# Last token tile of a decoder layer: the row store issued ahead of a ring load and of the h store

## What is computed

```
h  = x + concat(attn_o, conv_o) @ w_out
hn2 = rms_norm(h, ffn_norm_gain)
out = h + sum over a token's 2 experts e of  weight_e * ( (silu(hn2 @ w_gate[e]) * (hn2 @ w_up[e])) @ w_down[e] )
```

## Time and profile before

| what | value |
|---|---|
| median of 3 runs | 1155.69 us |
| the 3 runs | 1153.41 to 1156.58 us |
| the profiled execution, its time | 1153.28 us |
| the profiled execution, its span | 1151.4 us |
| TensorE busy | 1089.9 us (95%) |
| VectorE busy | 852.5 us (74%) |
| DMA, mean over the span | 220 GB/s |

### The profile page before, as it was taken

The page is one execution under the profiler, slowest core; times in us unless marked ns, Lnnn a source line. Parts: engine busy times, 40 slices in busy tenths (PEclk is TensorE's granted clock), DMA queues, the critical chain, the costliest instruction groups (busy, mean ns, idle before and its releaser), DMA issues.

```text
span 1151.4 us, 15392 instructions
## 1 busy us (share of the span) xinstructions
PE 1089.9 (95%) x5617; PEld 856.9 (74%) x5617; DVE 852.5 (74%) x1208; ACT 679.4 (59%) x1003; POOL 357.1 (31%) x433
## 2 busy tenths in 40 slices
PE   5999999999879998989799999999999999999996
PEld 4999999889758877767567777777777777766664
DVE  6645354454677776767788998988988989888894
ACT  7424232231465655543477787787877877777773
POOL 2323333233421111121214424434344344222221
PEclk9999999999999999999699999999999999999998
DMA  8021030302311222324899999999999999999972
GB/s 246 2 61 50 19 93 1 92 19 92 123 12 37 75 92 92 129 92 154 308 356 367 372 375 374 371 376 376 368 377 378 369 368 363 367 358 366 374 314 56
DMA packets 77403, 253.64 MB, mean 220 GB/s; under 512 B 18832, under 2 KB 43408, under 8 KB 52752
## 3 DMA queue, kind: packets, MB, share of 16 engines
q1 hardware_dynamic: 70160, 235.85, 55.1%
q0 software_dynamic: 7168, 16.79, 6.2%
HBM read 240.03 MB, written 20.97 MB: 227 GB/s over the span
## 4 chain that ended last, share of the span: by engine, by line
PE 46%; DMA 8%; DVE 4%; ACT 2%; issue 1%; POOL 1%; POOLq 0%; SPq 0%; ACTq 0%; DVEq 0%
PE banks L2123 9%; PE banks L2125 9%; PE banks L2124 9%; DMA raw<-in_w_gate 6%; PE banks L2142 4%; PE banks L2146 4%; PE banks L2144 4%; PE banks L2099 2%; PE banks L1659 1%; PE banks L1661 1%; PE banks L1660 1%; PE banks L2108 1%; DMA xn_rows<-hn 1%; DVE wlo L2043 1%; PE banks L1689 1%
## 5 line engine op out<-in xcount | busy, mean ns | idle before, releaser
L2043 DVE TENSOR_TENSOR wlo<-raw,whi 128x2048 fp32r<-128x2048 f32 x190 | 428.1, 2288 | 47.6 <-ACT whi L1992 47.4
L1992 ACT CAST whi<-raw 128x2048 fp32r<-128x2048 f32 x188 | 354.0, 1910 | 33.6 <-DMA raw<-in_w_gate 19.9
L1974 POOL DMA_INDIRECT out<-y_sb,table_i x32 | 152.7, 4772 | 195.4 <-ACT y_sb L2010 190.8
L2123 PE MATMUL banks<-whi,rT_hi 128*96 128x512 f32 x512 | 206.7, 404 | 3.2 <-DVE wlo L2043 2.5
L2125 PE MATMUL banks<-whi,rT_lo 128*96 128x512 f32 x512 | 203.0, 396 | 0.0
L2124 PE MATMUL banks<-wlo,rT_hi 128*96 128x512 f32 x512 | 201.8, 394 | 0.0
L2123 PEld LDWEIGHTS banks<-whi,rT_hi 128*96 128x96 f32 x512 | 83.0, 162 | 38.0 <-issue 3.3
L2125 PEld LDWEIGHTS banks<-whi,rT_lo 128*96 128x96 f32 x512 | 82.9, 162 | 36.4
L2124 PEld LDWEIGHTS banks<-wlo,rT_hi 128*96 128x96 f32 x512 | 83.4, 163 | 31.5
L1965 POOL DMA_INDIRECT rows<-xn_rows,table_i x30 | 48.9, 1630 | 180.8 <-PE banks L2099 173.2
L874 ACT ACTIVATE qk_sq<-banks 128x256 f32<-128x256 f32 x32 | 12.3, 385 | 128.9 <-PE banks L1517 128.9
(11 more groups left out here) (250 smaller groups left out, 2064.6 us busy)
## 6 DMA issues: line engine op xcount, KB each, us to landing
raw<-in_w_gate SPq DMA_DIRECT2D x64, 1024.0 KB, 22.9
raw<-in_w_up SPq DMA_DIRECT2D x64, 1024.0 KB, 23.2
raw<-in_w_down SPq DMA_DIRECT2D x64, 1024.0 KB, 24.4
c_raw<-in_w_in SPq DMA_DIRECT2D x12, 512.0 KB, 3.8
q_raw<-in_w_in SPq DMA_DIRECT2D x12, 512.0 KB, 6.1
x_stage<-in_x SPq DMA_DIRECT2D x8, 512.0 KB, 6.4
wo_raw<-in_w_out SPq DMA_DIRECT2D x2, 2048.0 KB, 7.7
h_sb<-in_x SPq DMA_DIRECT2D x8, 512.0 KB, 4.9
```

The costliest lines, as they stand in the source:

```text
L1974: pool.indirect_dma_start(out=s.out_rows, out_offset=bass.IndirectOffsetOnAxis(ap=s.table_i[:, e:e + 1], axis=0), in_=s.y_sb[e % 2][:], in ...
L1992: act.copy(s.w_hi[i % HI][:], s.raw[i % RING][:]).then_inc(s.hi_ready, 1)
L2043: dve.tensor_tensor(s.w_lo[i % RING][:], s.raw[i % RING][:], s.w_hi[i % HI][:].bitcast(F32), ALU.subtract).then_inc(s.lo_ready, 1)
L2123: pe.matmul(o, s.rT_hi[e % 2][:, c, :], hi[:, c4, :], start=(c == 0), stop=False)
```

## The change

In the last position (i = 7) SP's queue waits for `hn_ready` and stores `hn` first, then waits for the last part of the output projection and loads ring tile 11, and only then waits for `h_ready` and stores h. Before, the order was h store, tile 11, row store. For the other seven tiles nothing changes; no instruction is added or dropped, and GpSimd's waits are as they were.

```diff
@@ -658,13 +658,16 @@
                     sp.wait_ge(half_done, 4 * NT - 2)
                     for j in range(CONV_KEYS[0], CONV_KEYS[1]):
                         s.load_tile(sp, j)
+                if i == NT - 1:
+                    sp.wait_ge(hn_ready, 2 * NT)
+                    sp.dma_start(s.xn2_rows[t * P:(t + 1) * P, :], s.hn[:].rearrange("p c q -> p (c q)")).then_inc(hn_stored, 16)
+                    sp.wait_ge(half_done, 4 * NT)
+                    s.load_tile(sp, CONV_KEYS[1])
                 sp.wait_ge(h_ready, 2 * i + 2)
                 sp.dma_start(s.out_rows[t * P:(t + 1) * P, :], s.h_sb[b][:]).then_inc(h_stored[b], 16)
-                if i == NT - 1:
-                    sp.wait_ge(half_done, 4 * NT)
-                    s.load_tile(sp, CONV_KEYS[1])
-                sp.wait_ge(hn_ready, 2 * i + 2)
-                sp.dma_start(s.xn2_rows[t * P:(t + 1) * P, :], s.hn[:].rearrange("p c q -> p (c q)")).then_inc(hn_stored, 16)
+                if i < NT - 1:
+                    sp.wait_ge(hn_ready, 2 * i + 2)
+                    sp.dma_start(s.xn2_rows[t * P:(t + 1) * P, :], s.hn[:].rearrange("p c q -> p (c q)")).then_inc(hn_stored, 16)
```

## The result

| | before | changed |
|---|---|---|
| median of 22 runs | 1155.64 us (1152.46 to 1158.38) | 1158.10 us (1153.87 to 1161.08) |
| ratio, 95% interval | | 1.0023 (1.0014 to 1.0031) |
| profiled execution, time / span | 1153.28 / 1151.4 us | 1153.87 / 1152.0 us |

The forecast was 1155.7 us with a range to 1158.5, and no change within 0.3%. The kernel came out 0.23% slower, with medians 2.5 us apart: inside the range, but not nothing, and near the far end of rival two's price.

A forecast was written before the change was run, and what follows sets the result against it. The prediction took the chain to be mostly TensorE, with all engines waiting around 560 for expert 0's gather, held by queued DMA bytes. Its terms summed to 0.0 us, leaving 1155.7 us, range 1152.2 to 1158.5.

The forecast's parts named there:

- rival two: DMA line runs dry between tile 10 and the row store, last store late: 0.3 to 2.6 us slower, chance 0.11.
- The place: Handover around 560: a shift of expert 0's gather moves TensorE's start and passes to the end one for one.
- The issue stays at 553.04.: SP's row store still waits for hn, so its issue comes no earlier: no shift.
- The row store's landing: Row store lands right behind tile 10, at 557.7 instead of 561.4, 3.7 us earlier.
- The h store takes over the wait: GpSimd's wait before the first gather, still about 9.3 us, ends by the h store instead of the row store.
- The same bytes ahead of the last store: Last h store lands at 561.4, where the row store did; gather at 562.3, change 0.0 us.
- its bound without any overlap: Three moved transfers take lone times one after another from 553.04: 11.0 us, landing at 564.0, 2.6 us later.
- Rival one: h lands clear of tile 11, table releases gather 1.4 us earlier, clock may hold: 1.4 to 4.3 us faster, chance 0.09.
- The weighed page: On DMA completion order: no first-in first-out per issuing engine, but semaphore steps follow earlier writes of the same DMA engine.

The follow-up runs named there:

- the later ratios: The changed kernel timed again three times, no edit, against the kernel before: 0.9993, 1.0010 and 1.0000; against 0.999 for the unchanged kernel before, some 1.4 us.
- the control of the same group: The kernel before, no edit, timed again in the first and third of three groups against its other runs: ratios 0.9987 and 0.9990.

## Why the prediction was right, and where its size was off

- The place. Right: all that differs lies between the row store's issue and the first products. What follows the first product takes 580.9 to 583.9 us in the five traces with the old order (mean 582.1) and 581.1 to 582.9 in the four of the changed kernel (mean 581.9).
- "The issue stays at 553.04." Right within scatter: SP issues when hn is ready, in every trace.
- The row store's landing. Forecast 4.7 us after its issue, measured 3.8, and 3.6 to 3.8 in all four traces. Tile 10, behind which it stands, was down 2.3 to 2.6 us after that issue in three of them, where the forecast took over the 3.4 of the old order. h was issued 0.85 us after it, forecast about 0.9. Tile 11 was forecast 6.8 us after its own issue and took 6.9 in the first trace, but 9.5 and 9.3 in the second and third.
- The h store takes over the wait. Right, and shown from both sides: taking the wait away helps the changed order and not the old one.
- The same bytes ahead of the last store, "change 0.0 us". This is the term that was mis-sized. Bytes alone did not decide: with tile 11 between two stores issued at the last moment, the line ran at 246 to 348 GB/s for six microseconds, where before two were slow (254 and 336). Over the traces with either order the mean landing is 8.3 us before (8.4, 7.4, 9.2, 8.2, 8.3) and 9.7 us changed (8.6, 11.1, 10.9, 8.2), the mean handover 16.3 and 17.2 us. That is 0.9 us of handover from nine traces, between the 1.4 us of the later ratios and nothing, and the two orders overlap (15.7 to 18.0 us and 16.0 to 18.6), so nine traces do not settle it. The 2.5 us of the first comparison is the size of a late execution (18.5 against 16.0); that most of its 22 runs were late ones is not shown.
- Rival two had the right sign and price (0.3 to 2.6 us) but not the right mechanism: the line did not run dry, since the DMA share averages 0.95 while tile 11 moves; it ran slowly, and in two of four traces its end straggled. The range above 1155.7 us was built on that price, so it held partly by luck. The latest h store landed 11.1 us after the row store's issue, a little beyond the 11.0 that the forecast had as its bound without any overlap.
- Rival one's two halves, a gather released by the table and a clock that holds when TensorE's pause goes, are both seen with h early and tile 11 late. Its sum, 1.4 + 2.9 us, compares with 2.9 us of handover (16.3 to 13.4) and 2.4 us of faster first products there. The forecast's 2.9 was too high: it took the difference in length, 0.24 us a product, but the products overlap, and their starts are 0.43 us apart at the low clock and 0.23 at the high one. The medians show gains of 3.9 and 2.7 us against the control of the same group, and of 5.7 and 4.3 us against the other runs of the kernel before.
- The weighed page ("DMA: Bandwidth & Descriptors" of the Trainium skill, section "Queues, rings and completion order"): the side I took, that the h store's completion stays behind tile 11, agrees with the trace (561.8, then 563.1). In none of the three traces of the changed order that have both landings did h overtake it.

Why tile 11 is slow in this order stays open. With h issued 6.6 us ahead and tile 11 behind both stores it is not (373 to 467 GB/s from 554 to 559 in the first of those traces), with only the h store late it is not, and with both stores late it is, wherever tile 11 stands. Common to the slow cases is that nothing but the tail of tile 10 was queued when the stores were issued; that this is the cause was not tested.

The order h, row store, tile 11 beats both kernels: ratios 0.9956 and 0.9969, against 0.999 for the controls and 1.0023 and 1.0001 for the changed kernel.

## What to carry to other kernels

Before moving a transfer forward in a queue, list all that its consumer waits for. Here one of two awaited stores went ahead and the other behind a load, so the later of the two landed no earlier; the load alone had to go behind both. A store whose data were ready six microseconds early cost nothing when it was issued at once, and the order that did so and also kept the load behind both stores was the best one here.

## What the runs showed of the hardware

- A 1 MB load issued right behind a freshly issued 512 KB store ran at 246 to 348 GB/s for six microseconds (down to 221 in another trace); with a store ahead that had been queued for 6.6 us the same stretch ran at 373 to 467.
- One lagging engine of sixteen (DMA share 0.06 to 0.07 for 3 us) can follow such a stretch, and with it a store that lands 2.5 us late. It came in two of four traces of the changed order and in one of five of the old one.
- The gather of 96 rows took 4.2 to 6.8 us: 4.2 with tile 12 down 3.0 us after it left, 6.8 with tile 12 down only 6.0 us after and a lagging engine at its end, 4.7 to 6.0 with the old order.
- TensorE's granted clock stayed at 2.4 GHz into the first products when its pause between the fillers and the gathered rows was 0.5 us or less (three traces) and was at 1.2 GHz there behind pauses of 2.0 us and more (eleven traces).
